# One-hot matmuls and VectorE add the expert blocks' outputs into x, in place of a scatter to DRAM and a later combine

## The chip, the cores and the metric

The kernel runs on one core of one Trainium2 chip. The metric is the device time of one execution in microseconds (us); smaller is better.
## The reference

Two layers run over 512 tokens of 1024 float32 features. Each layer is a token mixer (retention in the first, a Conformer convolution in the second) and then a mixture of experts, which is where the change lies:

```python
lg = xt @ w_rg + b_rg ; g_idx = argmax(lg)                  # one of 4 groups, gate_g = its softmax value
top_v, top_i = lax.top_k(le_sel, 2) ; pe = softmax(top_v)   # two of the group's 8 experts
wts = gate_g * pe                                           # one weight per (token, choice)
yb[block] = (silu(xb @ w_gate[e]) * (xb @ w_up[e])) @ w_down[e]
out = segment_sum(yb * buf_w, buf_tok)                      # back to the tokens, weighted
x = x + out
```

Each of 32 experts has 6 MB of weights (gate and up in two slots of 2 MB, down in a third), all read once in each layer.

## The kernel before

**Blocks.** Each expert's tokens are cut into blocks of 32; an expert has at least one block. `cum` holds the running number of blocks, so `one_block` on PE runs in a hardware loop from `cum[e]` to `cum[e+1]`. With these inputs the first layer has 46 blocks and the second 48.

**Weights.** SP loads three slots for each expert into nine places, three experts deep (`places`, `slots_of`). A place is loaded again when PE has finished the last block of the expert that held it (SP waits on `gu_half`, `gu_mm` and `y_mm`). Nine slots are asked for before the first block of a stage.

**One block on PE** (L779 to L807), in program order: the gate and up products into bank 2 (64 matmul instructions in four column tiles of 32, two for each float32 product); `pick_rows`, which gathers the rows of the block after next into bank 6 with a one-hot matrix (32 instructions); a transpose of the activations `a_e`; `turn_block`, two transposes of the next block's gathered rows `hg`; and the down product into bank 4 (32 instructions). ScalarE takes silu of bank 2 (L541), copies the transposed activations (L543) and copies the block's output out of bank 4 (L546). VectorE multiplies into `a_e` (L1124), scales the next block's turned rows into `hgT` (`turned_block`, L1010), copies `hg` (`stage`, L1022) and makes the one-hot rows of a later block (`know_rows`, L998 to L1004).

**Output.** ScalarE's copy lies in one of eight places of `area_c`; POOL issues an indirect DMA for each block, which scatters 128 rows of 1 KB into `y_dram`, one row for a token, choice and quarter of features. Rows without a token point out of bounds and are dropped. When all scatters have landed, POOL raises `rows_out`, SP reads `y_dram` back in four tiles (L400), and `combine` on VectorE adds both choices of each token, weighted, into `x` (L1136, eight instructions of 128x1024), and the next norm follows tile by tile (`scale_norm` on VectorE, `norm_roots` on ScalarE: L502, L503, L951, L953 or L956).

**Router.** Before the blocks, VectorE works out one-hot choices, ranks and block numbers; two matmul groups on PE (L760 and L775) count and spread them; the combining weights are worked out last (L1113 to L1118).

## Time and profile before

| | us |
|---|---|
| median of 3 runs | 1688.78 |
| lowest, highest | 1684.76, 1690.64 |
| the profiled execution | 1690.58 |
| its span | 1688.7 |
| first expert stage: first block's matmul to the last output copy | 476.85 to 930.62 |
| second expert stage, likewise | 1197.32 to 1660.88 |
| from that last copy to the end of the span | 27.8 |

PE is busy for 85% of the span, but an engine's share of busy time is a mean over stages with different limits, and PE's busy time is modelled. The DMA row of the page tells more: the mean busy share of the 16 DMA engines is at its full value through both expert stages and low elsewhere. The two expert stages are 917 of 1689 us.

### The profile page before, as it was taken

To read this page: it belongs to the slowest core of one execution; us is meant where nothing else is said; L and a number is where in the kernel's file an instruction comes from. 1 tells how busy PE (TensorE), PEld (TensorE's weight loads), DVE (VectorE), ACT (ScalarE), POOL (GpSimd) and SP (SyncE) were. 2 spreads that over 40 slices of the span, in tenths; PEclk is the share of its full clock that TensorE was granted. 3 is DMA by queue.
4 is the path that set the end of the run, shared out by engine and by line. 5 is a ranking of instruction groups with operands and counts; after the bars stand their busy time and mean duration, and the time that the engine had idled before them with its cause. 6 is when DMAs were issued, how large, how long until landed. Compare 5 with 4: busy or idle time off the path is not lost. (4 is left out here: it accounts for less than half of the span.)

```text
span 1688.7 us, 38816 instructions
## 1 busy us (share of the span) xinstructions
PE 1442.3 (85%) x16208; PEld 941.4 (56%) x16209; DVE 498.7 (30%) x1197; ACT 458.4 (27%) x800; POOL 357.8 (21%) x291
## 2 busy tenths in 40 slices
PE   8999999999988889877688399889898886789882
PEld 6868678686645445434345288556554443445451
DVE  4222112221342212111021589943421211112124
ACT  4242422424312222211122332154222221122222
POOL 3434244343101011000010165512010100011100
PEclk9999999999999999989899599989999999999996
DMA  9212122121579999999999421036299999999995
GB/s 362 100 50 100 50 100 90 60 100 50 234 327 429 427 429 426 429 428 429 428 429 426 179 100 50 11 120 256 108 428 428 428 429 429 428 428 429 428 428 210
DMA packets 39319, 473.81 MB, mean 281 GB/s; under 512 B 6396, under 2 KB 6604, under 8 KB 10848
## 3 DMA queue, kind: packets, MB, share of 16 engines
q1 hardware_dynamic: 34512, 464.42, 65.9%
q0 software_dynamic: 4608, 8.41, 1.3%
q8 instruction: 44, 0.72, 0.2%
q10 hardware_dynamic: 144, 0.17, 0.0%
q14 instruction: 11, 0.09, 0.0%
HBM read 462.48 MB, written 14.68 MB: 283 GB/s over the span
## 5 line engine op out<-in xcount | busy, mean ns | idle before, releaser
L791 PE MATMUL ps<-ring,hgT 128*32 128x256 f32 x4160 | 257.9, 399 | 84.7 <-DMA ring<-w_gu 62.1
L433 POOL TENSOR_TENSOR w_lo<-ring,w_hi 128x512 fp32r<-128x512 f32 x176 | 238.5, 1358 | 378.7 <-ACT w_hi L509 378.6
L448 POOL DMA_INDIRECT y_dram<-area_c,idx_s x96 | 94.4, 983 | 760.0 <-ACT area_c L546 732.9
L791 PEld LDWEIGHTS ps<-ring,hgT 128*32 128x32 f32 x4160 | 144.5, 114 | 191.0 <-DMA ring<-w_gu 74.3
L509 ACT CAST w_hi<-ring 128x512 fp32r<-128x512 f32 x176 | 109.0, 626 | 352.6 <-PE ps L692 352.6
L1124 DVE TENSOR_TENSOR a_e<-sg_e,ps 128x128 f32<-128x128 f32 x94 | 27.1, 288 | 586.4 <-ACT sg_e L541 586.4
L732 PE MATMUL ps<-area_a,block_rows 128*32 128x256 f32 x3136 | 194.3, 388 | 2.3 <-DVE block_rows L1002 2.3
L732 PEld LDWEIGHTS ps<-area_a,block_rows 128*32 128x32 f32 x3136 | 110.8, 114 | 71.8 <-issue 14.2
L804 PE MATMUL ps<-ring,aT_e 128*32 128x256 f32 x2080 | 125.7, 382 | 18.5 <-DMA ring<-w_down 9.8
L541 ACT ACT_TABLE_LOAD x94 | 120.6, 1283 | 32.3 <-DVE wts L1118 30.7
L690 PE MATMUL ps<-w_hi,hT_hi 128*128 128x512 f32 x320 | 125.6, 392 | 2.9 <-DVE hT_lo L1303 2.9
L691 PE MATMUL ps<-w_lo,hT_hi 128*128 128x512 f32 x320 | 125.0, 391 | 0.0
L692 PE MATMUL ps<-w_hi,hT_lo 128*128 128x512 f32 x320 | 125.0, 391 | 0.0
L541 ACT ACTIVATE sg_e<-ps 128x128 f32<-128x128 f32 x94 | 26.2, 279 | 325.9 <-PE ps L791 325.9
L690 PE MATMUL ps<-hT_hi,w_hi 128*128 128x512 f32 x256 | 100.8, 394 | 3.2 <-POOL w_lo L433 2.5
L692 PE MATMUL ps<-hT_hi,w_lo 128*128 128x512 f32 x256 | 100.1, 391 | 0.0
L691 PE MATMUL ps<-hT_lo,w_hi 128*128 128x512 f32 x256 | 100.1, 391 | 0.0
L804 PEld LDWEIGHTS ps<-ring,aT_e 128*32 128x32 f32 x2080 | 62.9, 109 | 65.4 <-ACT aT_e L543 17.9
L546 ACT COPY area_c<-ps 128x256 f32 x94 | 35.1, 373 | 218.0 <-PE ps L804 215.8
L1010 DVE TENSOR_TENSOR hgT<-ps,par 128x128 f32<-128x128 f32 x192 | 46.9, 286 | 153.8 <-PE ps L741 153.8
L791 PE MATMUL ps<-area_b,hgT 128*32 128x256 f32 x928 | 61.6, 410 | 26.1 <-DMA area_b<-w_gu 26.1
L791 PE MATMUL ps<-area_c,hgT 128*32 128x256 f32 x928 | 56.9, 386 | 20.6 <-DMA area_c<-w_gu 14.8
(201 smaller groups left out, 1759.9 us busy)
## 6 DMA issues: line engine op xcount, KB each, us to landing
ring<-w_gu SPq DMA_DIRECT2D x88, 2048.0 KB, 34.2
ring<-w_down SPq DMA_DIRECT2D x44, 2048.0 KB
area_c<-w_gu SPq DMA_DIRECT2D x20, 2048.0 KB
area_b<-w_gu SPq DMA_DIRECT2D x20, 2048.0 KB
hT<-w_down SPq DMA_DIRECT2D x20, 2048.0 KB
ring<-w_pw SPq DMA_DIRECT2D x6, 2048.0 KB
ring<-w_qk SPq DMA_DIRECT2D x4, 2048.0 KB
ring<-w_v SPq DMA_DIRECT2D x4, 2048.0 KB
```

Source lines behind the costliest of these rows:

```text
L433: nc.gpsimd.tensor_tensor(w_lo[:, place, :], ring[:, s, at:at + 512], w_hi[:, place, :].bitcast(F32), ALU.subtract).then_inc(lo_ready, 1)
L448: pool.indirect_dma_start(y_dram[l], bass.IndirectOffsetOnAxis(ap=idx_s[:, b:b + 1].bitcast(U32), axis=0), y_out[:, b, :], None, bounds_ch ...
L509: nc.scalar.copy(w_hi[:, place, :], ring[:, s, at:at + 512]).then_inc(hi_ready, 1)
L541: nc.scalar.activation(sg_e[:, :], ps[:, 2, 0:P], ACT.Silu).then_inc(silu_ready[l], 1)
L546: nc.scalar.copy(area_c[:, bass.ds((t % GRP) * QW + 4096, QW)], ps[:, 4, 0:QW]) \
L690: nc.tensor.matmul(at, lhs[0], rhs[0], start=start, stop=False)
L691: nc.tensor.matmul(at, lhs[0], rhs[1], start=False, stop=False)
L692: return nc.tensor.matmul(at, lhs[1], rhs[0], start=False, stop=stop)
L732: last = nc.tensor.matmul(ps[32 * g:32 * g + 32, 6, 0:QW], block_rows[:, i, :], xn[:, i, g * QW:(g + 1) * QW], start=(i == 0), stop=(i == ...
L791: last = nc.tensor.matmul(ps[32 * g:32 * g + 32, 2, 0:256], hgT[:, n * (KT // 2) + k, :], gate_up[n][:, k, :, g * P:(g + 1) * P], start=(n ...
L804: last = nc.tensor.matmul(ps[32 * g:32 * g + 32, 4, 0:256], aT_e[:, k * BLK:(k + 1) * BLK], down[:, k, g * 256:(g + 1) * 256], start=(k == ...
L1010: ins = V.tensor_tensor(hgT[:, :, :].rearrange("p (q c) s -> p c q s", c=2)[:, c], ps[:, 1, c * P:(c + 1) * P].rearrange("p (q s) -> p q s ...
```

## The change

Nothing goes to DRAM any more. ScalarE rounds the weighted output of a block to fp32r (`y_hi`, scaled by the weight of each slot), VectorE makes the remainder (`y_lo`), and POOL makes a one-hot matrix `slot_tok` (32 slots by 512 tokens, four times on the partitions) from the token number of each slot. `put_rows` on PE multiplies the two: a half covers two tiles of 128 tokens, with 16 fp32r matmuls of 32 rows, 128 columns of weights and 256 moving columns, in four row tiles that write four different banks. VectorE adds the result from PSUM into `x` (`add_tile`, 128x1024, four for a block). A block's output is put in the next block: the first half behind gate and up, the second behind the transpose of `a_e` and ahead of `turn_block`. Both halves use banks 4 to 7, so the second waits until VectorE has taken the first two tiles. `pick_rows` is now one block ahead instead of two, and into bank 0. The router matmul at L775 spreads three columns (token number, high and low part of the weight) instead of one, and the weights are worked out before it.

```diff
@@ PE @@
+            def put_rows(half, bank, done):
+                for i in range(2):
+                    cols = slice((2 * half + i) * P, (2 * half + i + 1) * P)
+                    for n, part in enumerate((y_hi, y_lo)):
+                        for g in range(4):
+                            rows = slice(32 * g, 32 * g + 32)
+                            last = nc.tensor.matmul(ps[:, bank + g, i * QW:(i + 1) * QW], slot_tok[rows, cols],
+                                                    part[rows, :], start=(i == 0 and n == 0), stop=(i == 1 and n == 1),
+                                                    tile_position=(32 * g, 0))
+                last.then_inc(done, 1)
...
-                pick_rows(l, t + 2)
+                pe.wait_ge(y_split[l], t + 1)
+                pe.wait_ge(tok_hot[l], t + 1)
+                pe.wait_ge(added[l], 4 * t + 4)
+                put_rows(0, 4, first_mm[l])
+                pick_rows(l, t + 1)
                 pe.wait_ge(act_ready[l], t + 1)
                 nc.tensor.transpose(ps[:, 3, 0:P], a_e[:, :], ident).then_inc(t2_mm[l], 1)
+                pe.wait_ge(added[l], 4 * t + 6)
+                put_rows(1, 4, second_mm[l])
                 turn_block(l, t + 1)
...
+                total = pe.value_load(cum[0:1, NE:NE + 1], min_val=NE, max_val=NBLK - 1)
+                pe.wait_ge(y_split[l], total + 1)
+                pe.wait_ge(tok_hot[l], total + 1)
+                pe.wait_ge(added[l], 4 * total + 4)
+                put_rows(0, 0, first_mm[l])
+                put_rows(1, 4, second_mm[l])
@@ POOL @@
-                    pool.indirect_dma_start(
...
+                with pool.Fori(0, total) as t:
+                    pool.wait_ge(tok_hot[l], t + 1)
                     pool.nop(nofuse=True)
+                    pool.tensor_copy(slot_now[:, :], slots[:, bass.ds(t, 1)]).then_inc(slot_known[l], 1)
+                    pool.wait_ge(slot_known[l], t + 1)
+                    pool.wait_ge(second_mm[l], t + 1)
+                    pool.nop(nofuse=True)
+                    nc.gpsimd.tensor_scalar(slot_tok[:, :], tok_number, slot_now[:, 0:1], None,
+                                            ALU.is_equal).then_inc(tok_hot[l], 1)
@@ ACT @@
                     act.wait_ge(y_mm[l], t + 1)
-                    act.wait_ge(y_free[l], t + 1)
-                    nc.scalar.copy(area_c[:, bass.ds((t % GRP) * QW + 4096, QW)], ps[:, 4, 0:QW]) \
-                        .then_inc(y_ready[l], 1)
+                    act.wait_ge(second_mm[l], t + 1)
+                    nc.scalar.activation(y_hi[:, :], ps[:, 3, P:P + QW], ACT.Copy,
+                                         scale=slots[:, bass.ds(t + NBLK, 1)]).then_inc(y_rounded[l], 1)
@@ DVE, a block @@
-                    dve.wait_ge(gu_mm[l], t + 1)
+                    dve.wait_ge(first_mm[l], t + 1)
+                    add_tile(0, 4).then_inc(added[l], 1)
+                    add_tile(1, 4).then_inc(added[l], 1)
+                    stage(l, t + 1)
+                    dve.wait_ge(second_mm[l], t + 1)
+                    add_tile(2, 4).then_inc(added[l], 1)
                     turned_block(l, t + 1, gain)
-                    stage(l, t + 2)
-                    know_rows(l, t + 3)
+                    add_tile(3, 4).then_inc(added[l], 1)
+                    dve.wait_ge(y_rounded[l], t + 1)
+                    V.scalar_tensor_tensor(out=y_lo[:, :], in0=ps[:, 3, P:P + QW],
+                                           scalar=slots[:, bass.ds(t + NBLK, 1)], in1=y_hi[:, :].bitcast(F32),
+                                           op0=ALU.mult, op1=ALU.subtract).then_inc(y_split[l], 1)
+                    know_rows(l, t + 2)
@@ DVE, behind the blocks @@
                 for i in range(NT):
-                    dve.wait_ge(y_loaded[l][i], 16)
-                    for k in range(2):
-                        ins = V.scalar_tensor_tensor(out=x[:, i, :], in0=ytile[i][:, k * D:(k + 1) * D],
...
-                    if i > 0:
-                        scale_norm(n, [i - 1])
-                scale_norm(n, [NT - 1])
+                    if i % 2 == 0:
+                        dve.wait_ge(second_mm[l] if i else first_mm[l], total + 1)
+                    dve.wait_ge(added[l], 4 * total + (i + 1))
+                    add_tile(i, 4 if i > 1 else 0).then_inc(combined, 1)
+                    if i > 1:
+                        scale_norm(n, [i - 2])
+                scale_norm(n, [NT - 2, NT - 1])
@@ PE, behind the first layer's blocks @@
+            pe.wait_ge(combined, NT)
             turn_norm(2)
@@ SP @@
+                sp.wait_ge(idx_mm[l], 1)
+                sp.dma_start(tok_number, tok_in.partition_broadcast(P)).then_inc(tok_loaded[l], 16)
...
-                sp.wait_ge(rows_out[l], 1)
-                for i in range(NT):
-                    sp.dma_start(ytile[i], y_dram[l].rearrange("(t r) c -> t (r c)", r=8)[i * P:(i + 1) * P, :]) \
-                        .then_inc(y_loaded[l][i], 16)
```

What PE has in one block, in program order. Before (`ps<-ring,hgT` is gate and up, `area_a,block_rows` the gathering, `ring,aT_e` down; a float32 product counts once here and twice in the trace):

```order
L791 MATMUL ps<-ring,hgT 32x256 x32
L727 REGISTER_ALU
L729 REGISTER_ALU
L732 MATMUL ps<-area_a,block_rows 32x256 x16
L798 MATMUL ps<-const,a_e 128x128
L741 MATMUL ps<-const,hg 128x128 x2
L804 MATMUL ps<-ring,aT_e 32x256 x16
```

And with the change (`slot_tok` with `y_hi` and `y_lo` are the two halves of `put_rows`):

```order
L764 MATMUL ps<-ring,hgT 32x256 x32
L771 ISA
L747 MATMUL ps<-y_hi,slot_tok 128x256 x4
L747 MATMUL ps<-y_lo,slot_tok 128x256 x4
L747 MATMUL ps<-y_hi,slot_tok 128x256 x4
L747 MATMUL ps<-y_lo,slot_tok 128x256 x4
L689 REGISTER_ALU
L694 MATMUL ps<-area_a,block_rows 32x256 x16
L775 MATMUL ps<-const,a_e 128x128
L776 REGISTER_ALU
L747 MATMUL ps<-y_hi,slot_tok 128x256 x4
L747 MATMUL ps<-y_lo,slot_tok 128x256 x4
L747 MATMUL ps<-y_hi,slot_tok 128x256 x4
L747 MATMUL ps<-y_lo,slot_tok 128x256 x4
L703 MATMUL ps<-const,hg 128x128 x2
L783 MATMUL ps<-ring,aT_e 32x256 x16
```

The first half of 16 now stands between gate and up and the gathering, the second between the transpose of `a_e` and that of `hg`; nothing else changes places.

What VectorE has in one block, before:

```order
L1124 TENSOR_TENSOR a_e<-sg_e,ps 128x128
L1008 REGISTER_ALU
L1010 TENSOR_TENSOR hgT<-ps,par 128x4x32 x2
L1021 REGISTER_ALU
L1022 COPY hg<-ps 128x256
L997 ISA
L998 TENSOR_TENSOR both_hot<-const,pos 128x256
L1001 REGISTER_ALU
L1002 TENSOR_TENSOR block_rows<-both_hot 128x128
L1004 TENSOR_SCALAR pos<-pos 128x8
```

And with the change (`x<-x,ps` is `add_tile`):

```order
L1128 TENSOR_TENSOR a_e<-sg_e,ps 128x128
L1120 TENSOR_TENSOR x<-x,ps 128x1024 x2
L1007 REGISTER_ALU
L1008 COPY hg<-ps 128x256
L1120 TENSOR_TENSOR x<-x,ps 128x1024
L996 TENSOR_TENSOR hgT<-ps,par 128x4x32 x2
L1120 TENSOR_TENSOR x<-x,ps 128x1024
L1138 ISA
L1138 SCALAR_TENSOR_TENSOR y_lo<-ps,slots,y_hi 128x256
L983 ISA
L984 TENSOR_TENSOR both_hot<-const,pos 128x256
L987 REGISTER_ALU
L988 TENSOR_TENSOR block_rows<-both_hot 128x128
L990 TENSOR_SCALAR pos<-pos 128x8
```

`hg` is now copied before `hgT` is made, `hgT` stands behind three of the four additions, and `block_rows` behind all of them and `y_lo`.

## Rows read from the trace of the kernel before

**Rows 1.** The page: mean busy share of the DMA engines in 40 slices.
```profile
DMA  9212122121579999999999421036299999999995
```

**Rows 2.** Windows of both expert stages: us, DVE busy of L1124 (x), PEclk, DMA share, GB/s.
```profile
476.00:931.00 455.00, 13.27 (x46) 0.96 1.00 424
1197.00:1662.00 465.00, 13.84 (x48) 0.97 0.95 403
```

**Rows 3.** Timeline of one block: start us, us, engine line op out<-in xcount [idle before <-releaser].
```profile
1255.09 3.64 PE L791 MATMUL ps<-ring,hgT 128*32 128x256 f32 x64
1255.47 0.37 ACT L546 COPY area_c<-ps 128x256 f32 x1 [2.18 <-PE ps L804]
...
1258.55 1.91 PE L732 MATMUL ps<-area_a,block_rows 128*32 128x256 f32 x32
...
1259.11 0.29 DVE L1124 TENSOR_TENSOR a_e<-sg_e,ps 128x128 f32<-128x128 f32 x1 [4.31 <-ACT sg_e L541]
...
1260.55 0.38 PE L741 MATMUL ps<-const,hg 128*128 128x128 f32 x2
...
1260.97 0.49 DVE L1010 TENSOR_TENSOR hgT<-ps,par 128x128 f32<-128x128 f32 x2 [1.57 <-PE ps L741]
1261.07 1.93 PE L804 MATMUL ps<-ring,aT_e 128*32 128x256 f32 x32
...
1262.82 3.64 PE L791 MATMUL ps<-ring,hgT 128*32 128x256 f32 x64
```

**Rows 4.** Timeline of PE: at a change of expert, and over a third expert of three.
```profile
1229.81 1.93 PE L791 MATMUL ps<-area_c,hgT 128*32 128x256 f32 x32 [0.47 <-issue]
...
1238.71 1.59 PE L791 MATMUL ps<-ring,hgT 128*32 128x256 f32 x24 [0.97 <-issue]
...
1271.20 1.93 PE L791 MATMUL ps<-area_c,hgT 128*32 128x256 f32 x32 [0.47 <-issue]
```

**Rows 5.** Small and whole tiles (one line's busy us in all), and DVE's additions from PSUM.
```profile
L910 PE MATMUL ps<-area_b,area_a 32*32 32x512 f32 x1024 | 34.3, 596 | 0.0
...
1055.74 0.23 PEld L910 LDWEIGHTS ps<-area_b,area_a 32*32 32x32 f32 x32 [0.35 <-issue]
...
474.68 0.97 PEld L775 LDWEIGHTS ps<-block_hot_r,slot_hot_r 128*128 128x128 f32 x8 [0.94 <-DVE block_hot_r L1100]
...
444.69 2.48 DVE L1221 TENSOR_TENSOR x<-x,ps 128x512 f32<-128x512 f32 x4 [8.60 <-PE ps L692]
```

**Rows 6.** Timeline of DVE in the router of the first expert stage.
```profile
464.75 0.19 DVE L1065 TENSOR_SCALAR area_c<-ps 128x32 int32<-128x32 f32 x1 [1.30 <-PE ps L762]
...
473.87 0.76 DVE L1100 TENSOR_TENSOR block_hot_r<-area_c,const 128x576 fp32r<-128x576 f32 x1
...
476.50 0.16 DVE L1113 TENSOR_REDUCE area_c<-small 128x4 f32<-128x16 f32 x1
...
477.53 0.16 DVE L1118 TENSOR_TENSOR wts<-wts,small 128x4 f32<-128x4 f32 x1
```

**Rows 7.** Timeline behind the last block of the first expert stage.
```profile
930.62 0.37 ACT L546 COPY area_c<-ps 128x256 f32 x1 [2.18 <-PE ps L804]
...
958.18 3.27 PEld L668 LDWEIGHTS ps<-const,area_a 128*128 128x128 f32 x16 [1.80 <-DVE area_a L953]
...
960.40 1.84 ACT L515 ACTIVATE hT_hi<-ps,par 128x512 fp32r<-128x512 f32 x3 [1.62 <-PE ps L668]
```

**Rows 8.** Timeline behind the last block of the second expert stage.
```profile
1660.88 0.37 ACT L546 COPY area_c<-ps 128x256 f32 x1 [2.18 <-PE ps L804]
...
1673.15 1.28 ACT L503 ACT_TABLE_LOAD   x1
...
1684.42 1.28 DVE L956 SCALAR_TENSOR_TENSOR area_a<-x,small,trig 128x1024 f32<-128x1024 f32 x1
```

**Rows 9.** Lines of POOL: out<-in shapes xcount | busy us, mean ns | idle before.
```profile
L433 POOL TENSOR_TENSOR w_lo<-ring,w_hi 128x512 fp32r<-128x512 f32 x176 | 238.5, 1358 | 378.7 <-ACT w_hi L509 378.6
...
L458 POOL TENSOR_TENSOR area_c<-area_c 128x512 f32<-128x512 f32 x1 | 20.0, 19955 | 17.1 <-ACT area_c L640 17.1
```

More of the change, by code:

```diff
@@ L160, in program @@
         slot_hot_r = over("slot_hot_r", [P, 8, P], trig_at, 0)
-        block_hot_r = over("block_hot_r", [P, 8, NBLK], area_c_at, route_at)
+        block_hot_r = over("block_hot_r", [P, 3, 8, NBLK], area_c_at, route_at)
+        y_hi = over("y_hi", [P, QW], area_c_at, route_at)
+        y_lo = over("y_lo", [P, QW], area_c_at, route_at + QW)
+        slot_tok = over("slot_tok", [P, S], area_c_at, route_at + 2 * QW)
         ident = const[:, C_ID:C_ID + P]
@@ L213, in program @@
             [area_c[:, 0:SLOT], area_b[:, 0:SLOT], hT[:, :, :].rearrange("p k s -> p (k s)")]
-        gfin = trig[:, :, :].rearrange("p a s -> p (a s)")
-        y_out = area_c[:, 4096:4096 + GRP * QW].rearrange("p (b c) -> p b c", b=GRP)
-        y_dram = [nc.dram_tensor(f"y_dram{l}", [8 * S, QW], F32, kind="Internal").ap() for l in range(NL)]
+        gfin = bias_2[:, :]
+        tok_number = trig[:, 0, :]
         slot_loaded = sems("slot_loaded", 3 * DEPTH)
@@ L228, in program @@
         gfin_loaded = sem("gfin_loaded")
-        y_loaded = [sems(f"y_loaded{l}_", NT) for l in range(NL)]
         out_stored = sem("out_stored")
@@ L731, in pick_rows @@
                     for g in range(4):
-                        last = nc.tensor.matmul(ps[32 * g:32 * g + 32, 6, 0:QW], block_rows[:, i, :],
+                        last = nc.tensor.matmul(ps[32 * g:32 * g + 32, 0, 0:QW], block_rows[:, i, :],
                                                 xn[:, i, g * QW:(g + 1) * QW],
@@ L803, in one_block @@
                     for g in range(4):
[L804 removed]
+                        last = nc.tensor.matmul(ps[32 * g:32 * g + 32, 3, P:P + QW], aT_e[:, k * BLK:(k + 1) * BLK],
                                                 down[:, k, g * 256:(g + 1) * 256],
@@ L1102, in route @@
+                turned_block(l, 0, gain)
+                link.done(V.tensor_tensor(block_hot_r[:, 1], block_hot[:, :, :],
+                                          coef[:, 1, :].unsqueeze(2).to_broadcast([P, 8, NBLK]), ALU.mult))
+                V.tensor_tensor(block_hot_r[:, 2], block_hot[:, :, :],
+                                coef[:, 2, :].unsqueeze(2).to_broadcast([P, 8, NBLK]), ALU.mult) \
                     .then_inc(spread_ready[l], 1)
-                stage(l, 1)
-                know_rows(l, 2)
+                know_rows(l, 1)
@@ new lines, in route @@
+                link.sent(V.tensor_tensor(slots[:, NBLK:2 * NBLK], slots[:, NBLK:2 * NBLK], ps[:, 7, NBLK:2 * NBLK],
+                                          ALU.add))
+                link.done(V.tensor_copy(slots[:, 0:NBLK], ps[:, 7, 0:NBLK]))
+                V.sem_inc(idx_ready[l], 1)
+                link.sent(V.tensor_scalar(y_hi[:, :], const[:, 0:QW], 0.0, None, ALU.mult))
+                link.sent(V.tensor_scalar(y_lo[:, :], const[:, 0:QW], 0.0, None, ALU.mult))
+                link.done(V.tensor_scalar(slot_tok[:, :], const[:, 0:S], 0.0, None, ALU.mult))
```

138 lines of the change are left out of this document (50 added, 88 removed).

## The prediction

> **What bounds the kernel now.** I read the page first. The DMA row stands at its full value in two long plateaus and low elsewhere [rows 1]. The windows of these two stages, the expert stages, have a DMA share of 1.00 and 0.95, while VectorE's one multiplication for each block shows 46 blocks in the first and 48 in the second [rows 2]. Then I read the timeline of blocks that have their weights. One lasts from 1255.09 to 1262.82, which is 7.73 us: gate and up 3.46, gathering to turn 2.00, then the short wait for the turned activations, and down from 1261.07, 1.75 [rows 3]. A change of expert adds 0.65 (from 1262.82 to 1271.20 is 8.38), and every third one 1.17 (from 1229.81 to 1238.71 is 8.90) [rows 3, 4]. A stage with 31 changes, ten of them of the long kind, so has 21 x 0.65 + 10 x 1.17 = 25.4 us of them.
>
> The first stage has 46 x 7.73 + 25.4 + 0.38 (to the output copy, 1255.09 to 1255.47 [rows 3]) = 381 us of PE's own pace, but takes 453.8 (476.85 to 930.62). The second has 397 and takes 463.6 (1197.32 to 1660.88). So about 72 and 67 us are waits for weights. The transfers set the end of both stages, and a block may grow by 72/46 = 1.57 and 67/48 = 1.39 us before PE sets it instead. This is the number that decides: the change puts matmuls and additions into each block, and takes work out behind each stage.
>
> **The price of a block with the change.** All times run from the first gate matmul.
>
> A half of put_rows has 16 fp32r matmuls, 256 columns each, in four row tiles. The trace has no such tile. What is near: 16 tiles of 32x32 ran 1024 matmuls in 34.3 us, 33 ns each, and 32 of their weight loads started within 0.13 us (0.23 less one's 0.10), so loads into different tiles do not queue for each other there [rows 5]. At 33 ns a half is 0.53. The lower end is loads and matmuls of four tiles wholly beside each other, one load of 0.11 (0.97 less one's 0.19, over 7) for four matmuls: 0.45 [rows 5]. The upper end is one whole load for each matmul: 16 x 0.11 = 1.8 [rows 5]. I take 0.55, next to the small tiles.
>
> The Trainium skill, "TensorE: Matmul & The Clock Gate", section "LDWEIGHTS (loading the stationary operand)", speaks against this: a load costs by its columns, so 32 rows by 128 columns cost what the whole array costs, and the 32 columns of the small tiles say nothing for 128. If the loads also queue, that is the upper end, and rival 1 below.
>
> An addition is 128x1024 from PSUM. Four of 512 took 2.48 [rows 5], so 0.60 from start to start, 0.53 of it for 512 elements; with 1024 it is 1.13, and 1.21 for one alone.
>
> The chain: gate and up end at 3.45, the tile shape changes (I estimate 0.15 to 0.2 from the step gathering to transpose), the first half runs 3.63 to 4.15. Its last result is there 0.2 behind that (gate and up last 3.64 where the next matmul starts at 3.46 [rows 3]) and, with 0.1 for the wait, VectorE adds tile 0 from 4.48 and has tile 1 done at 6.83; a_e (at 4.02 to 4.31, by 1259.11 in rows 3) just fits before. PE meanwhile gathers (1.83) and transposes until about 6.4, and waits: the second half needs the banks that tiles 0 and 1 leave. It runs 6.95 to 7.48. Then two ways are equally long. PE: change of shape, two transposes, change, down 1.75, next block at 9.7. VectorE: third addition 7.8 to 8.9, hgT 0.49 [rows 3], the wait's 0.1, 9.5. So **9.7 us for a block, 1.97 more**. The fourth addition, y_lo and know_rows fall into the next block's gate and up (until about 2.3 of 3.45); ScalarE's y_hi takes the place of its copy. POOL's one-hot has from 7.8 to 13.3, and a POOL operation of 128x512 has 1.36 [rows 9]: hidden. I cost these at nothing. If any fails to fit, it lengthens each block by its excess.
>
> The Trainium skill, "TensorEngine Tiling (Array Packing)", section "Key Properties", says that a change of tiling mode drains TensorE. A block has four changes more than before (gate to put, put to gather, and on both sides of the second half). In rows 3 gathering and turn are 2.00 apart where 32 matmuls of 54 ns take 1.74 and the transpose of a_e comes between: a change is at most 0.15 or so there, already in the chain. With a full 0.3 for each by that rule a block would have 0.3 to 0.4 more and the time would be some 30 us above the sum.
>
> **Both stages.** First: 46 x 1.97 = 90.6 less 72.4 of waits that close = +18.2. Second: 48 x 1.97 = 94.6 less 66.8 = +27.8. At this pace PE is behind the transfers, which also lose the scatter's bytes, so I leave no waits in.
>
> **Router.** Six small instructions (476.50 to 477.53, 0.2 each) and four like them move ahead of the count, 2.1 us, of which the wait of 1.30 there covers part: +0.85. Two more products of 0.7 ahead of the spread, against know_rows (1.0) gone from there: +0.45 [rows 6]. So +1.3 in each stage.
>
> **Behind the stages.** From the last output copy before: 960.40 - 930.62 = 29.8 to the next mixer's first operand [rows 7], and 1688.7 - 1660.88 = 27.8 to the end. After: y_hi and y_lo 0.85, a half and its result 0.9, three additions to 5.2; the square, table load (1.28 [rows 8]) and root of tile 0 end at 5.9, its norm at 6.8, the fourth addition at 8.0. In the first layer 32 transposes follow, 0.2 each as in 3.27 for 16 [rows 7], the 25th at 13.3, and the operand at 14.1: -15.7. At the end of the kernel four norms of 1.28 follow instead [rows 8], the last ends at 13.1 where 1684.42 + 1.28 - 1660.88 = 24.8 stood: -11.7. The scatter and the reading back are gone from these stretches.
>
> **Sum.** 18.2 + 27.8 + 2 x 1.3 - 15.7 - 11.7 = +21.2 us on the profiled execution of 1690.6, which is 1711.8. That execution is 1.8 above the median of the runs; I predict **1711**. All of it hangs on the block: 94 blocks make 94 us for each us, and the balance is at 9.47 us for a block.
>
> **Rivals.**
> 1. *Weight loads queue* (slower by far). A half is 1.8. The first half then ends at 5.45, tile 1 is added at 8.1, the second half ends at 10.0, hgT and down at about 12.2: 2.5 more for each block, 94 x 2.5 = 235, some 1945 us. For it: whole-array loads stand 0.11 apart. Against: the small tiles' 32 loads in 0.23 us.
> 2. *The transfers still set the end* (faster). It decides from a block of 9.4 us or less. With halves of 0.45 and changes of shape at 0.05 the chain is about 9.25 to 9.3. At 9.3 the sum is 21.2 - 94 x 0.4 = -16, 1674 us; the removed waits, writes and reads then stay gained. At the very best, with no PE limit at all, it would be the two ends behind the stages less the router's 2.6, -24.8, and the scatters' 8192 rows of 1 KB at the 424 GB/s of rows 2, -20: some -45. For it: every end that I rounded. Against: VectorE's three additions and hgT alone, with gate and up, two halves and the results' ways, are 9.2.
> 3. *The one-hot comes late.* One POOL operation on SBUF took 20.0 us where the mean of others is 1.36 [rows 9]. If VectorE's additions hold POOL off, it starts behind y_lo, at about 11 to 12, and ends at or just above the 13.3 at which the next first half wants it: up to 0.3 for each block, 1739 us. Against: the additions have one operand in PSUM.
>
> **How the numbers follow.** The forecast has 0.58 (blocks of 9.45 to 10.3, mostly above 9.5), rival 1 and half-way cases 0.14, rival 2 0.20, rival 3 0.08. A measurement of this kernel can tell 0.3%, 5 us, from no change: blocks of 9.41 to 9.52. From these: faster 0.20, same 0.08, slower 0.72. The range goes from 1672 (a block of 9.3) to 1780 (10.4); it leaves out the rest of rival 2 and most of rival 1. The forecast's own range is 1695 to 1760.
>
> **What would show it.** Blocks that have their weights stand 9.7 apart, with PE idle about 0.5 before the second half, released by an addition. Halves last about 0.55. The DMA share of the expert stages falls below 1 and SP's loads are issued late, held by PE. Behind the last block the operand comes 14 us after the copy. I am wrong if blocks with weights stand under 9.4 apart, or if halves last over 0.8, or if PE still waits for weights at most changes of expert.

## The result and the profile after

The changed kernel takes 1700.7 us in the median of four runs (1697.1 to 1703.2), the kernel before 1688.4 (four runs). The ratio is 1.008, with a 95% interval of 1.006 to 1.010: slower by 0.8%. The forecast was 1711, slower, with a range of 1672 to 1780. In medians the change costs 12.3 us. The profiled execution of the changed kernel took 1697.1 us, 6.5 more than that of before; it is the shortest of its four, and the kernel before was profiled (1690.6) at the upper end of its own, so an account by the two profiles falls some 6 us short of the medians.

The page of the changed kernel: busy time, share and instructions of the engines, then the DMA engines in 40 slices.

```profile
PE 1558.8 (92%) x19216; PEld 1012.7 (60%) x19217; DVE 968.7 (57%) x1669; ACT 467.1 (28%) x800; POOL 425.1 (25%) x371
...
DMA  9212122121679998999999121135399999999892
```

PE was at 85% and is at 92, DVE was at 30% and is at 57. The two plateaus of the DMA row have slices under 9 now, which they had not in [rows 1]. The two expert stages as windows, with the columns of [rows 2] (VectorE's busy time is that of L1128, which is L1124 of before):

```profile
476.00:931.00 455.00, 12.97 (x45) 1.00 0.98 414
1197.00:1679.00 482.00, 13.84 (x48) 1.00 0.90 379
```

The DMA share was 1.00 and 0.95 [rows 2] and is 0.98 and 0.90: the same weights come over a longer time, and the scatters' bytes are gone. What PE waited for in the second expert stage (1190 to 1679), in us, times and the longest:

```profile
PE ps L764 <- issue: 19.9, 31, 1.1
PE ps L747 <- DVE x L1120: 16.1, 48, 0.3
```

Not one wait for weights is left, and the same view of the first stage lists none either. The 31 of the first row are the changes of expert, 0.64 each in the mean; the 48 of the second row are the wait before the second half of `put_rows`, one for each block. Now one block in the timeline (start us, us, engine line operation, what ended the idle time before):

```profile
1212.58 3.64 PE L764 MATMUL ps<-ring,hgT 128*32 128x256 f32 x64
1212.94 0.47 ACT L511 ACTIVATE y_hi<-ps,slots 128x256 fp32r<-128x256 f32 x1 [3.18 <-PE ps L783]
...
1216.15 0.39 PE L747 MATMUL ps<-y_hi,slot_tok 32*128 32x256 f32 x4
...
1216.37 0.29 PE L747 MATMUL ps<-y_lo,slot_tok 32*128 32x256 f32 x4
...
1216.49 0.29 PE L747 MATMUL ps<-y_hi,slot_tok 32*128 32x256 f32 x4
...
1216.61 0.28 PE L747 MATMUL ps<-y_lo,slot_tok 32*128 32x256 f32 x4
...
1216.83 1.93 PE L694 MATMUL ps<-area_a,block_rows 128*32 128x256 f32 x32
1216.95 2.35 DVE L1120 TENSOR_TENSOR x<-x,ps 128x1024 f32<-128x1024 f32 x2
...
1218.69 0.33 PE L775 MATMUL ps<-const,a_e 128*128 128x128 f32 x1
...
1219.36 0.39 PE L747 MATMUL ps<-y_hi,slot_tok 32*128 32x256 f32 x4 [0.34 <-DVE x L1120]
...
1220.03 0.44 PE L703 MATMUL ps<-const,hg 128*128 128x128 f32 x2
1220.16 1.22 DVE L1120 TENSOR_TENSOR x<-x,ps 128x1024 f32<-128x1024 f32 x1 [0.52 <-PE ps L747]
1220.28 1.56 POOL L455 TENSOR_SCALAR slot_tok<-trig,slot_now 128x512 fp32r<-128x512 f32 x1 [7.62 <-PE ps L747]
...
1220.40 1.93 PE L783 MATMUL ps<-ring,aT_e 128*32 128x256 f32 x32
...
1222.50 0.47 ACT L511 ACTIVATE y_hi<-ps,slots 128x256 fp32r<-128x256 f32 x1 [3.18 <-PE ps L783]
```

ScalarE's copy of the output (`y_hi`) stands at 1212.94 and again at 1222.50, so the block lasts 9.56 us, where one with its weights lasted 7.73 [rows 3]. A half runs in four rounds of four matmuls: 0.22 us from the first round to the second, 0.12 to each of the next two, and 0.22 from the last to the gathering, 0.68 in all (1216.15 to 1216.83). The two additions behind the first half end at 1219.30, and the second half has waited 0.34 for them. POOL's one-hot starts right behind the second half.

**Where the time went, stage by stage, in the two profiled executions:**

| stretch | before | after | difference | forecast |
|---|---|---|---|---|
| start to the first gate matmul | 476.85 | 474.27 | -2.6 | +1.3 |
| first expert stage, to its last output copy | 453.8 | 466.9 | +13.1 | +18.2 |
| from there to the second one's first gate matmul | 266.7 | 250.05 | -16.65 | -14.4 |
| second expert stage | 463.6 | 488.0 | +24.4 | +27.8 |
| end of the span | 27.8 | 16.0 | -11.8 | -11.7 |
| sum | | | +6.5 | +21.2 |

The rows at the end of the kernel show the last term. Before it was [rows 8].

```profile
1679.19 0.47 ACT L511 ACTIVATE y_hi<-ps,slots 128x256 fp32r<-128x256 f32 x1 [3.19 <-PE ps L783]
...
1681.33 3.48 DVE L1120 TENSOR_TENSOR x<-x,ps 128x1024 f32<-128x1024 f32 x3 [0.29 <-PE ps L747]
...
1690.88 1.29 DVE L942 SCALAR_TENSOR_TENSOR area_a<-x,small,bias 128x1024 f32<-128x1024 f32 x1
```

The last norm ends 13.0 us behind the copy of the output; it was 24.8.

### The profile page after: what moved, and what is told of

Its sections match the earlier page's. It is cut to its first block, busy times and chain, and to the rows that moved or that the text cites. A ratio compares the mean times of both kernels' runs of the same rounds, so it can differ in the third digit from the quotient of the medians.

```text
span 1695.2 us, 46059 instructions
## 1 busy us (share of the span) xinstructions
PE 1558.8 (92%) x19216; PEld 1012.7 (60%) x19217; DVE 968.7 (57%) x1669; ACT 467.1 (28%) x800; POOL 425.1 (25%) x371
## 4 chain that ended last, share of the span: by engine, by line
PE 76%; DVE 11%; issue 9%; ACT 2%; POOL 1%; DMA 0%; DVEq 0%; SPq 0%; ACTq 0%; POOLq 0%
PE ps L764 20%; PE ps L783 10%; PE ps L652 10%; PE ps L653 10%; PE ps L654 10%; PE ps L747 8%; DVE x L1120 7%; PE ps L703 2%; PE ps L848 2%; POOL area_c L439 1%; PE ps L896 1%; PE ps L840 1%; PE ps L916 0%; PE ps L710 0%; ACT area_a L467 0%
## 5 line engine op out<-in xcount | busy, mean ns | idle before, releaser
L1120 DVE TENSOR_TENSOR x<-x,ps 128x1024 f32<-128x1024 f32 x384 | 459.0, 1216 | 55.2 <-PE ps L747 49.1
L455 POOL TENSOR_SCALAR slot_tok<-trig,slot_now 128x512 fp32r<-128x512 f32 x94 | 147.0, 1564 | 761.6 <-PE ps L747 761.6
L764 PE MATMUL ps<-ring,hgT 128*32 128x256 f32 x4160 | 240.3, 383 | 29.9 <-issue 29.8
L694 PE MATMUL ps<-area_a,block_rows 128*32 128x256 f32 x3072 | 185.7, 382 | 2.6 <-DVE block_rows L988 2.6
L1128 DVE TENSOR_TENSOR a_e<-sg_e,ps 128x128 f32<-128x128 f32 x94 | 27.1, 288 | 226.8 <-ACT sg_e L506 226.8
L747 PE MATMUL ps<-y_hi,slot_tok 32*128 32x256 f32 x1536 | 120.1, 328 | 34.4 <-DVE x L1120 31.6
L694 PEld LDWEIGHTS ps<-area_a,block_rows 128*32 128x32 f32 x3072 | 90.4, 109 | 65.9 <-issue 4.2
L747 PEld LDWEIGHTS ps<-y_hi,slot_tok 32*128 32x128 f32 x1536 | 73.9, 182 | 91.9 <-DVE x L1120 53.3
L511 ACT ACTIVATE y_hi<-ps,slots 128x256 fp32r<-128x256 f32 x94 | 44.6, 475 | 298.8 <-PE ps L783 298.8
L747 PE MATMUL ps<-y_lo,slot_tok 32*128 32x256 f32 x1536 | 100.0, 275 | 0.0
L508 ACT COPY aT_e<-ps 128x128 f32<-128x128 f32 x94 | 25.1, 267 | 234.3 <-PE ps L775 234.3
```

The costliest lines, as they stand in the source:

```text
L455: nc.gpsimd.tensor_scalar(slot_tok[:, :], tok_number, slot_now[:, 0:1], None, ALU.is_equal).then_inc(tok_hot[l], 1)
L694: last = nc.tensor.matmul(ps[32 * g:32 * g + 32, 0, 0:QW], block_rows[:, i, :], xn[:, i, g * QW:(g + 1) * QW], start=(i == 0), stop=(i == ...
L747: last = nc.tensor.matmul(ps[:, bank + g, i * QW:(i + 1) * QW], slot_tok[rows, cols], part[rows, :], start=(i == 0 and n == 0), stop=(i == ...
L764: last = nc.tensor.matmul(ps[32 * g:32 * g + 32, 2, 0:256], hgT[:, n * (KT // 2) + k, :], gate_up[n][:, k, :, g * P:(g + 1) * P], start=(n ...
L1120: return V.tensor_tensor(x[:, i, :].rearrange("p (g c) -> p g c", g=4), x[:, i, :].rearrange("p (g c) -> p g c", g=4), ps[:, bank:bank + 4 ...
```

## The experiments

Eleven kernels ran, each beside the kernel before on the same chip. The length of an expert stage is read in the same way in all: from the start of its first silu (`sg_e` on ScalarE) to that of its last. By this measure the stages are 445.6 and 455.5 us before and 456.4 and 475.8 after the change.

### Is the wait for weights slack?

Two kernels from the one before, with `k` = 1 and 2:

```
                 pick_rows(l, t + 2)
+                stay_awake(5, k)
```

> The kernel before with one idle matmul of 512 columns (about 0.85 us, its result is never read) added behind the gather in each block. The sum of the forecast rests on slack: TensorE waits 1.57 us (first expert stage) and 1.39 us (second) a block for weights, so that work of less than that added to a block costs nothing. By it this kernel takes 1688 to 1692 us. Rival (the wait for weights is no slack: work added delays the freeing of a ring place and so the loads): up to 94 x 0.85 = 80 us more, 1768 us.

> The kernel before with two idle matmuls of 512 columns (about 1.71 us together) added behind the gather in each block, which is just over the slack of 1.57 and 1.39 us a block. By the forecast's account only what exceeds the slack costs: 46 x 0.14 + 48 x 0.32 = 6 + 15 = 21 us, 1710 us (1700 to 1725, since the slack is not spread evenly). Rival (no slack): 94 x 1.71 = 160 us more, 1849 us. Rival (slack larger than read, since TensorE could run up to the rate of the transfers): no change, 1690.

Measured: with one, 1689.2 us, ratio 1.001 (0.9999 to 1.0021); with two, 1715.9, ratio 1.017 (1.016 to 1.019). Stages 447.5 and 455.3, then 454.7 and 473.9. A block with one idle matmul and with its weights lasts 8.64 us (1255.68 to 1264.32 in its timeline), 0.91 more than before. With two it lasts 9.52, 1.79 more and not the 1.71 that I expected:

```profile
1258.87 3.66 PE L791 MATMUL ps<-ring,hgT 128*32 128x256 f32 x64 [0.48 <-issue]
...
1268.39 3.64 PE L791 MATMUL ps<-ring,hgT 128*32 128x256 f32 x64
```

So 0.91 us more work in each of 94 blocks costs nothing that can be measured, and 1.79 us cost 29 instead of 94 x 1.79 = 168. The waits of PE for weights show why. With one idle matmul, first stage (476 to 934), the largest of them:

```profile
PE ps L791 <- DMA ring<-w_gu: 18.3, 9, 3.4
```

All waits for weights that this view lists are 26 us there, where they were 62 before (of the 72 that the prediction worked out; where the rest lies was not traced). With two, the same stretch:

```profile
PE ps L791 <- issue: 19.9, 31, 1.0
PE ps L791 <- DMA area_b<-w_gu: 0.9, 1, 0.9
```

The slack is real, and it has the size that was worked out. With 1.79 instead of 1.71 the account gives 46 x (1.79 - 1.57) + 48 x (1.79 - 1.39) = 10 + 19 = 29 us, and 29 was measured (the stages grow by 9.1 and 18.4): the 21 expected were too few because of the size of the idle work and not because of the slack. And once the waits for weights are gone, the length of a block sets that of a stage: blocks of 9.52 us make 454.7 and 473.9 here, blocks of 9.56 make 456.4 and 475.8 in the changed kernel.

### Is the changed kernel without slack?

Eight more matmuls ahead of those of the gathering, in `pick_rows` of the changed kernel:

```
+                for i in range(2):
+                    for g in range(4):
+                        nc.tensor.matmul(ps[32 * g:32 * g + 32, 0, QW:2 * QW], block_rows[:, i, :],
+                                         xn[:, i, g * QW:(g + 1) * QW],
+                                         start=(i == 0), stop=(i == 1), tile_position=(0, 32 * g))
```

> The changed kernel with eight more matmuls of 256 columns in each gather (16 instructions of 58 ns, 0.93 us on TensorE; their result is never read). They stand between the first put and T, where TensorE in the changed kernel waits 0.34 us a block later on. If the changed kernel is bound by TensorE's own chain: 0.93 - 0.34 (the wait is used up) = 0.59 us a block, 94 x 0.59 = +55 us, 1755 us. If VectorE's chain or nothing is covered: +87 us, 1787 us. If the kernel still had slack as before (where an idle matmul of 0.85 us cost 2 us): under 1710 us.

Measured: 1745.0 us, 1.032 of before (1.031 to 1.034), 44 more than the changed kernel. Two blocks of it:

```profile
1293.28 3.64 PE L769 MATMUL ps<-ring,hgT 128*32 128x256 f32 x64
...
1303.30 3.64 PE L769 MATMUL ps<-ring,hgT 128*32 128x256 f32 x64
```

A block is 10.02, 0.46 longer. The extra matmuls take 0.88 (1254.79 to 1255.67 in its timeline) and 0.41 of that goes into the time from T to the second half, which falls from 0.67 to 0.26. 94 x 0.46 = 43. I expected 55: the extra work is a little shorter than 0.93, and 0.41 of it is covered and not 0.34. Of about the same work that made 2 us of difference before the change, the part that no wait covers now counts in full.

### What do the halves and the wait cost?

Without the low part of `y`, in `put_rows`:

```
-                    for n, part in enumerate((y_hi, y_lo)):
+                    for n, part in enumerate((y_hi,)):
```

> The changed kernel with the products of the low part y_lo left out of both puts (8 of 16 matmuls of each half; the output lacks that part, all waits stay). If the puts lie on the chain that sets the end, two rounds of four matmuls at 0.117 us go from each half: 0.47 us a block, to 9.1 us, and the kernel to 1700 - 94 x 0.47 = about 1656 us (1653 to 1668, transfers limiting at some changes). Rival (the puts run beside the wait for additions or for weights, so that their length is hidden): within 5 us of the changed kernel. If only one of the two puts counts (the second lies behind a wait for additions that would grow by what the first gives): half of it, about 1678 us.

Measured: 1665.2 us, 0.987 of before (0.986 to 0.989), 35 less than the changed kernel. One block, with half of the matmuls in each half:

```profile
1300.37 0.51 PE L747 MATMUL ps<-y_hi,slot_tok 32*128 32x256 f32 x8
...
1303.41 0.51 PE L747 MATMUL ps<-y_hi,slot_tok 32*128 32x256 f32 x8 [0.41 <-DVE x L1120]
...
1309.54 0.51 PE L747 MATMUL ps<-y_hi,slot_tok 32*128 32x256 f32 x8
```

The block is 9.17. Each half gives 0.24, but the wait before the second grows from 0.34 to 0.41: 0.39 a block, not 0.47. 94 x 0.39 = 37.

Without the additions of tiles 0 and 1 in the loop:

```
-                    add_tile(0, 4).then_inc(added[l], 1)
-                    add_tile(1, 4).then_inc(added[l], 1)
+                    V.sem_inc(added[l], 2)
```

> The changed kernel without the additions of row tiles 0 and 1 inside the loop over blocks (the output of those rows is left out; the second stage's routing of them may differ, so the first expert stage and the length of a block are what is compared). Theory: TensorE's 0.34 us wait ahead of the second put is for exactly these additions, so the block goes from 9.56 to about 9.2 us and the first stage from 466.9 to about 451 us. Rival (the additions are on the chain through VectorE as well, hg, add of tile 2, hgT, so that each addition's 1.2 us counts): a block of 8.9 us or less, or transfers of weights as the new limit. Rival (the wait moves to another releaser, such as hg for the turn): block 9.5 us.

Measured: the second stage has 49 blocks there, so its total (1677.4 us) says little. The block, from one start of gate and up to the next:

```profile
1260.89 3.64 PE L764 MATMUL ps<-ring,hgT 128*32 128x256 f32 x64
...
1266.99 0.33 PE L775 MATMUL ps<-const,a_e 128*128 128x128 f32 x1
1267.25 0.39 PE L747 MATMUL ps<-y_hi,slot_tok 32*128 32x256 f32 x4
...
1270.04 3.64 PE L764 MATMUL ps<-ring,hgT 128*32 128x256 f32 x64
```

9.15 us, 0.41 less, all of it between T and the second half (0.67 to 0.26). The first stage takes 443.3 instead of 456.4, 13 less where 46 x 0.41 = 19; of the rest 3.8 are waits for weights that come back, and some 2 were not traced. It is the wait that counts in a block, not the 2.4 us of additions behind it.

### What were the scatters worth?

The kernel before with `scatter(b)` and the waits for it taken out of POOL's loop (the last eight blocks of a stage are still scattered, behind it), and `ytile` loaded from `w_gu0` instead of `y_dram`:

```
                         pool.nop(nofuse=True)
-                        scatter(b)
                         if b == GRP - 2:
-                            pool.wait_ge(scattered_lo[l], 8 * GRP * g + 8 * GRP)
```

> The kernel before without the scatters of the blocks inside the loop (only the last eight blocks of a stage are scattered, and the rows read back come from a weight array of the same size, so the output and the second stage's routing are not the reference's; the first expert stage is what is compared). It asks what the scatters' 8.4 MB cost the expert stages that wait for weights. By the forecast's rival 2: at 424 GB/s they are 10 us in each stage, the first goes from 453.8 to about 444 us and the kernel to about 1670. Rival A (a transfer in the queue of the scatters takes more than its bytes, 1 KB rows against 16 KB ones): 435 us or less in the first stage. Rival B (the scatters lie in gaps of the weights' transfers): 453 us, 1687 us for the kernel.

Measured: 1679.2 us, 0.994 of before (0.992 to 0.996), with 49 blocks in the second stage. The first takes 435.8 instead of 445.6, 9.8 less. The indirect DMAs of both stages fall from 8.41 to 0.47 MB, which makes 4.0 MB a stage and 9.4 us at 424 GB/s: the scatters cost about their bytes. The whole kernel gains no more than 10, and not the 20 expected, since the last eight scatters now stand one behind the other after the last block (1641.91 to 1651.94), so that 37.2 us pass from the last output copy to the end instead of 27.8. So some 10 us a stage are what the transfers gave back, and what the changed kernel, bound by PE, doesn't collect.

### Can the wait be filled?

The order of TensorE in a block, in four versions. The first has down, turn and the second half last:

```
-                pe.wait_ge(added[l], 4 * t + 6)
-                put_rows(1, 4, second_mm[l])
-                turn_block(l, t + 1)
...
+                turn_block(l, t + 1)
+                pe.wait_ge(added[l], 4 * t + 6)
+                put_rows(1, 4, second_mm[l])
```

> The changed kernel with TensorE's order of a block turned round behind T: down, then the turn, then the second put last; VectorE writes the operand hgT ahead of the additions of row tiles 2 and 3. Nothing is left out. My account of the changed kernel: a block is a serial chain on TensorE of 9.56 us, of which 0.34 us is a wait for an addition ahead of the second put, since nothing else stands there. With the 1.7 us of down between T and the second put that wait is covered, so a block comes to about 9.2 us and the kernel to 1700 - 94 x 0.34 = about 1668 us, between 1665 and 1680 if transfers now limit at some changes of expert. Rival A (the kernel is held by VectorE's additions or by the transfers of weights, and the order on TensorE doesn't matter): within 5 us of the changed kernel, 1696 or more. Rival B (late additions of tiles 2 and 3 push y_lo and so the next block's first put): a new wait ahead of the first put, no gain or a loss, 1700 or more.

Measured: 1772.4 us, 1.050 of before (1.048 to 1.052). My theory gave 1668. Rival B allowed for a loss, but by a wait before the first half that isn't there. A block and a change of expert in it:

```profile
1251.55 3.66 PE L764 MATMUL ps<-ring,hgT 128*32 128x256 f32 x64
...
1257.67 0.33 PE L775 MATMUL ps<-const,a_e 128*128 128x128 f32 x1
1258.44 1.93 PE L780 MATMUL ps<-ring,aT_e 128*32 128x256 f32 x32 [0.43 <-ACT aT_e L508]
...
1262.65 3.66 PE L764 MATMUL ps<-ring,hgT 128*32 128x256 f32 x64 [1.23 <-issue]
```

The wait for the addition is gone, but in its place stands one for `aT_e`: T to down is 0.77, which the second half used to cover. The block is 9.86 (1241.69 to 1251.55). And the changes of expert now idle PE for 43.0 us in the first stage and 43.3 in the second (1225 to 1760), where the changed kernel has 19.6 and 19.9. So 94 x 0.30 = 28, 23 and 23 make 74; measured 72.

The second version puts T ahead of the gathering, and keeps down, turn and second half behind it:

```
+                pe.wait_ge(act_ready[l], t + 1)
+                nc.tensor.transpose(ps[:, 3, 0:P], a_e[:, :], ident).then_inc(t2_mm[l], 1)
                 pick_rows(l, t + 1)
```

> The changed kernel with TensorE's order of a block: first put, T ahead of the gather, gather, down, turn, second put last; VectorE writes hgT ahead of the additions of tiles 2 and 3. Nothing is left out. In the run with down first, T stood just before down and the wait for aT_e (0.75 us from T's start to down's start) took the place of the wait for an addition, and TensorE's idle time at a change of expert was 1.36 us instead of 0.64. Theory: both waits inside the block are covered here, so a block is 3.57 + 0.68 + 0.15 + 1.87 + 1.87 + 0.37 + 0.73 = about 9.25 us, but the short instructions of a put still stand last before a change of expert, which then costs about 1.36 + 0.3 us each: 94 x (9.25 - 9.56) = -29 and 62 x 0.72 = +45, so about 1716 us (1705 to 1722). Rival (the 1.36 us belong to something else in the run with down first, and only the block's chain counts): 1700 - 29 = 1671 us.

Measured: 1718.2 us, 1.017 of before (1.015 to 1.018), as the theory had it. Its changes of expert in the first stage:

```profile
PE ps L764 <- issue: 42.6, 31, 1.8
```

The third gathers one block further ahead and puts that last (T, down and second half stand for their lines, which are the same):

```
                 put_rows(0, 4, first_mm[l])
-                pick_rows(l, t + 1)
                 T
-                second half
                 turn_block(l, t + 1)
                 down
+                second half
+                pick_rows(l, t + 2)
```

> The changed kernel with the gather a block further ahead and last: first put, T, turn of t+1, down, second put, gather of t+2; VectorE writes hgT before it waits for the second put and copies hg of t+2 behind y_lo. Nothing is left out; two more instructions groups (a gather and a copy) move into the router. Theory: the gather's 1.87 us stands last, so that a change of expert costs what it does in the changed kernel (0.64 us idle), and no addition is waited for; T to down is covered by the turn but for about 0.3 us. Block 3.57 + 0.68 + 0.15 + 0.37 + 0.3 + 1.75 + 0.68 + 1.87 = 9.35 us or less: 94 x -0.2 to -0.3 = -19 to -28, so 1672 to 1682 us, under both kernels. Rival A (the change of expert costs the same 1.36 us whatever stands last): 1700 - 25 + 45 = 1720 us. Rival B (transfers now set the end): PE waits for weights and 1685 or more.

Measured: 1684.6 us (six runs), 0.997 of before (0.996 to 0.998). First stage, changes of expert and the waits beside them:

```profile
PE ps L765 <- issue: 20.6, 32, 1.0
PE ps L781 <- DMA hT<-w_down: 1.8, 1, 1.8
PE ps L765 <- DMA area_b<-w_gu: 1.1, 1, 1.1
```

The change of expert is back at 0.64. The block is 9.33 (5.76 from the first half to the next gate and up, 1257.84 to 1263.60, and 3.57), which would give 22; measured 16 in medians. Weights are waited for again, 2.9 us in the first stage, whose gain is 5.5 (450.9); the second's is 9.6 (466.2).

The fourth puts the turn ahead of T and a quarter of the gathering between T and down:

```
+                turn_block(l, t + 1)
                 T
-                turn_block(l, t + 1)
+                pick_part(l, t + 2, [0])
                 down
                 second half
-                pick_rows(l, t + 2)
+                pick_part(l, t + 2, [1, 2, 3])
```

> The kernel with the gather last, changed once more: turn ahead of T, and a quarter of the gather of t+2 (four of sixteen matmuls, 0.47 us) between T and down, where TensorE waited 0.38 us for aT_e; the wait of 0.33 us for a_e ahead of T is covered by the turn. Nothing is left out. Theory: a block goes from 9.33 to about 9.1 us. In the second stage that is 48 x 0.2 = 10 us; in the first the transfers ran at a share of 1.01 from 700 to 925 us already, so that less comes of it, 0 to 9 us. 1684.6 less 10 to 19: 1666 to 1675 us, under all others that compute the whole. Rival (the transfers limit both stages): 1680 to 1684. Rival (the shorter gather, 1.4 us last, no longer covers the change of expert): a part of the 0.72 us a change comes back, 1690 or more.

Measured: **1665.6 us** (1664.9 to 1666.2), 0.986 of before (0.985 to 0.988), a little under what was expected. It computes the whole result and beats both kernels, the changed one by 35 us. Three first halves in a row, with a change of expert before the third:

```profile
1253.19 0.39 PE L759 MATMUL ps<-y_hi,slot_tok 32*128 32x256 f32 x4
...
1262.20 0.39 PE L759 MATMUL ps<-y_hi,slot_tok 32*128 32x256 f32 x4
...
1262.87 0.44 PE L714 MATMUL ps<-const,hg 128*128 128x128 f32 x2
1263.15 0.27 PE L787 MATMUL ps<-const,a_e 128*128 128x128 f32 x1
1263.35 0.64 PE L691 MATMUL ps<-area_a,block_rows 128*32 128x256 f32 x8
1263.81 1.91 PE L793 MATMUL ps<-ring,aT_e 128*32 128x256 f32 x32
...
1268.35 1.93 PE L776 MATMUL ps<-area_c,hgT 128*32 128x256 f32 x32 [0.53 <-issue]
...
1271.94 0.39 PE L759 MATMUL ps<-y_hi,slot_tok 32*128 32x256 f32 x4
```

No matmul here waits for another engine. A block without a change lasts 9.01 us (1253.19 to 1262.20), the one with a change 9.74. Windows in its stages (us, busy us and instructions of PE, PEld, DVE, ACT, POOL, then PEclk, DMA share, GB/s):

```profile
700.00:925.00 225.00, 209.91 (x3705) 120.43 (x3701) 153.53 (x272) 51.21 (x91) 38.52 (x45) 0.99 1.01 427
1190.00:1420.00 230.00, 219.03 (x3900) 125.28 (x3904) 162.75 (x286) 55.21 (x96) 41.92 (x48) 1.00 0.95 401
```

The first stage takes 440.2, within 5 of the 435.8 of the kernel before without scatters, the DMA share is 1.01 from 700 to 925, and PE waits for weights again, 5.6 us in all: the transfers and PE are now about even there.

The last kernel asks what makes the change of expert dear when a half of `put_rows` stands last. It is the second version with eight idle matmuls behind the second half:

```
                 put_rows(1, 4, second_mm[l])
+                for i in range(2):
+                    for g in range(4):
+                        nc.tensor.matmul(ps[32 * g:32 * g + 32, 0, QW:2 * QW], ident[:, 0:BLK],
+                                         xn[:, i, g * QW:(g + 1) * QW],
+                                         start=(i == 0), stop=(i == 1), tile_position=(0, 32 * g))
```

> The kernel with the order T, gather, down, turn, second put (1718 us) with eight idle matmuls of 256 columns (0.88 us, their result is never read) added behind the second put, at the end of each block. In that kernel TensorE idled 1.37 us at each of the 31 changes of expert of a stage (42.6 us), in the changed kernel 0.64 us; the difference is that 0.7 us of a put stand last instead of 1.75 us of down. Theory: what TensorE has still queued covers the branch and the reading of registers, so the idle time at a change falls by up to the added 0.88 us, to 0.64 or a little less, and costs no more than in the changed kernel: 94 x 0.88 = +83 and 62 x -0.7 = -43, so 1718 + 40 = 1758 us (1750 to 1768). Rival (the idle time at a change has a fixed length behind the last matmul and depends on what kind of instruction it follows): 1.37 stays, 1718 + 83 = 1801 us.

Measured: 1780.8 us, 1.055 of before (1.053 to 1.057), between both expectations. Its changes of expert in the first stage:

```profile
PE ps L764 <- issue: 32.7, 32, 1.4
```

1.02 each, between 0.64 and 1.37. So 0.88 us of work behind the half hides 0.35 of the change, not all that it could. With down or the gathering last it was 0.64 to 0.68 in three orders, with a half last 1.37 to 1.39 in two, so what stands last does move this cost; how PE's sequencer and its queue share the time is not shown, and stays open. The last 1.4 us of the fourth version hide as much as the 1.75 of down.

## Why the prediction was right, point by point

**The balance decides.** Right, and now shown from both sides: 0.9 us more a block are free before the change (1.001) and 0.88 us cost 44 us after it. The change ate the slack of 1.57 and 1.39 us and went over it by 0.26 and 0.44 us a block, 33 us in all, of which what it saves behind the stages pays the larger part.

**The price of a block, +1.97.** It was +1.83. From the first gate matmul, measured and (forecast): the first half starts at 3.57 (3.63), the additions at 4.37 (4.48), the second half at 6.78 (6.95), the turn at 7.45, the next block at 9.56 (9.7). So the mis-sized term is the way from gate and up to the additions, 0.11 shorter, and then the step from the second addition to the second half, 0.06 (1219.30 to 1219.36) instead of 0.12. The halves were well sized: with the change of shape on both sides one takes 0.79 of PE's time (0.11 more from gate and up than to the gathering in [rows 3], and 0.68), where the forecast had 0.52 and twice 0.15 to 0.2. PE's wait is 0.34 and not 0.5, since the second half comes earlier. The 0.14 too much are 13 us over 94 blocks; 21.2 less 13 is 8, and 6.5 was measured on the profiled executions. In medians the forecast was +22 and +12.3 was measured, so by them the block takes 13 off and 3 us are left the other way. (The forecast's 1711.8 less 1.8 is 1710, not 1711.) Leaving out the additions (9.15 us a block) and the low products (9.17) shows that both lie on this chain.

**The stages, +18.2 and +27.8.** Measured +13.1 and +24.4. 46 x 9.56 + 25.4 + 0.36 (first gate matmul to the copy) = 465.5 against 466.9; 48 blocks give 484.6 against 488.0, of which 2.2 are the stage's first gate and up:

```profile
1191.22 5.87 PE L764 MATMUL ps<-ring,hgT 128*32 128x256 f32 x64
```

It took 3.66 before. From 1191.2 to 1197.2 TensorE's granted clock was 0.62, a mean of the two levels 1.2 and 2.4 GHz, and in the same place before (1197.3 to 1203) it was 1.00. Ahead of it PE had waited 1.31, 1.33 and 2.08 us for VectorE in the new router; before, no wait for VectorE there was over 0.91. With the same waits the first stage began at 0.85, with a gate and up of 4.26. The forecast has no such term. For the rest the arithmetic of blocks and changes holds.

**Router, +1.3 each.** The first gate matmul came 2.6 earlier instead of 1.3 later, of which 3.2 are gained ahead of the router: the additions of the mixer that stood at 444.69 before [rows 5] stand at 441.47. The change doesn't touch that code, and the runs show that it is a difference between executions and no gain of the change: with the router of before, the kernels with one and two idle matmuls and the one without scatters start these additions at 442.4, 442.2 and 442.0 and the first gate matmul at 474.7, 474.3 and 474.2. The profiled execution of before was the late one. From these additions to the first gate matmul 32.2 us pass in all four with the old router (32.15 to 32.26) and 32.8 in the changed kernel, so the router costs 0.6 and not 1.3. Which of the small instructions hide was not traced.

**Behind the stages, -15.7 and -11.7.** Measured -16.65 with the second router in it (forecast -14.4) and -11.8. The chain of three additions, root, norm, fourth addition came as worked out, each 0.2 to 0.4 later (behind the first stage's copy at 941.17 they end at 5.6, 6.1, 7.1 and 8.3, forecast 5.2, 5.9, 6.8 and 8.0). The next mixer's operand follows at 13.2 instead of 14.1: the 32 transposes took 5.6 us, where 0.2 each would be 6.4.

**The signs.** Blocks stand 9.56 apart for 9.7, PE idles 0.34 for 0.5 before the second half and an addition ends it, and the DMA share fell below 1. That SP's loads are held by PE says nothing: SP waited for PE's products of the blocks for 752 us before and 792 after.

**Rival 1, weight loads queue:** refuted. Four loads of 32 by 128 run within 0.19 us together, 0.182 to 0.184 each by themselves:

```profile
1216.26 0.19 PEld L747 LDWEIGHTS ps<-y_lo,slot_tok 32*128 32x128 f32 x4
```

The rule of the Trainium skill, "TensorE: Matmul & The Clock Gate", section "LDWEIGHTS (loading the stationary operand)", holds for one load: with the same 128 columns, a load for 32 rows takes 0.18 and one for the whole array 0.19 [rows 5]. Four loads into different row tiles lie beside each other in this trace, and that kept the half at 0.68 instead of 1.8. So what one load costs decides nothing about the rival.

**Rival 2, the transfers still set the end:** it needed a block of 9.4 or less. The changed kernel missed that by 0.16. The gain that this rival held is there: the fourth order has it, with 1665.6 us and a block of 9.01. For 9.3 us a block I gave 1674 (by the median 1672, since the sum stands on an execution 1.8 above it); the third order has blocks of 9.33 and took 1684.6.

**Rival 3, the one-hot comes late:** refuted. It starts 0.92 behind the second half's first matmul and takes 1.56, and ends 4 us before it is wanted:

```profile
L455 POOL TENSOR_SCALAR slot_tok<-trig,slot_now 128x512 fp32r<-128x512 f32 x94 | 147.0, 1564 | 761.6 <-PE ps L747 761.6
```

**The change of shape.** By the Trainium skill, "TensorEngine Tiling (Array Packing)", section "Key Properties", a change of tiling mode drains TensorE. With 0.3 each I had 30 us more as its price; the 0.3 was a guess of mine, the section gives no size. From gate and up to a half 0.11 more pass than to the gathering before the change, the first round is 0.22 long instead of 0.12, and from the last round to the gathering 0.22 pass, 0.10 more than a round takes. That is 0.31 for the two changes around a half, about 0.15 each: what the chain had, and half of 0.3. In the last kernel 0.22 pass, too, from the last round of the second half to the idle matmuls (1255.82 to 1256.04), where no wait and no register stands between, so these 0.10 are not a wait for a semaphore. That the cost is a drain is not shown. At a change of shape the load of the weights starts with its matmul (1216.82 and 1216.83), and without one 0.2 ahead of it (1212.37 and 1212.58).

## What to carry to other kernels

Work put into a loop whose transfers set the pace is free up to the slack, and costs its full length behind it. So work out the slack per pass first, test it with idle work of that length (measure the idle work in the trace, here it was 1.79 us and not 1.71), and then ask whether the waits between engines in the new order add up to more than it. When a serial chain waits for another engine, look for work in the loop that can stand there, from the next pass if need be; but check each neighbour that the moved piece used to cover, and what stands last before a branch. Here the same instructions took 1772, 1718, 1701, 1685 and 1666 us in five orders.

## What the runs showed of the hardware that I had not expected

- fp32r matmuls of 256 columns with a 32-row contraction in four row tiles take 0.12 us for each round of four, loads of 128 columns included, though one such load takes 0.18 by itself.
- PE's idle time between two inner loops (the changes of expert) depends on what stands last in its body: 0.64 us with 1.75 us of matmuls behind the last wait, 1.37 with 0.7 us, 1.02 with 1.6 us.
- After waits of 1.31, 1.33 and 2.08 us for VectorE in the router, TensorE's granted clock was 0.62 at the start of the second stage and 0.85 at that of the first, and the first gate and up took 5.87 and 4.26 us instead of 3.66.
- An addition of 128x1024 with one operand in PSUM takes 1.22 us on DVE, and two in a row 2.35; POOL's one-hot of 128x512 takes 1.56, where its subtraction of that shape took 1.36 [rows 9].
